# Attention copies per head and ahead of the exponentials, and a shorter routing chain in front of the experts

## The reference, cut to what matters

```python
def attend(q, k, v):
    s = jnp.einsum('bqhgd,bkhd->bhgqk', q, k) * scale
    p = softmax_f32(s).astype(v.dtype)
    return jnp.einsum('bhgqk,bkhd->bqhgd', p, v)
```

```python
p_group = jax.nn.softmax(tf @ w_rg.astype(jnp.float32) + b_rg.astype(jnp.float32), axis=-1)
pg, gsel = lax.top_k(p_group, 1)
...
le_g = jnp.einsum('tge,tg->te', le, jax.nn.one_hot(gsel[:, 0], MOE_GROUPS, dtype=jnp.float32))
pe = jax.nn.softmax(le_g, axis=-1)
pv, pi = lax.top_k(pe, EXPERT_TOPK)
wts = pg * pv / jnp.sum(pv, axis=-1, keepdims=True)
```

## Time and profile before

| | us |
|---|---|
| median of 3 runs | 2212.93 |
| lowest and highest run | 2212.61, 2214.05 |
| the profiled execution | 2210.14 |
| its span, first to last instruction | 2208.2 |
| PE busy in the span | 2006.7 |

### The profile page before, as it was taken

The page is one execution under the profiler, slowest core; times in us unless marked ns, Lnnn a source line. Parts: engine busy times, 40 slices in busy tenths (PEclk is TensorE's granted clock), DMA queues, the critical chain, the costliest instruction groups (busy, mean ns, idle before and its releaser), DMA issues.

```text
span 2208.2 us, 27501 instructions
## 1 busy us (share of the span) xinstructions
PE 2006.7 (91%) x10057; PEld 1407.3 (64%) x10057; DVE 1040.5 (47%) x2098; ACT 559.3 (25%) x1112; POOL 60.0 (3%) x69
## 2 busy tenths in 40 slices
PE   6999898789959999979978989999999878999997
PEld 4888686557736555545445468888544455678886
DVE  3456571356332222243666777777688234423311
ACT  3334300152021111131156033332000224434410
POOL 0000000000001000000000000101000010000000
PEclk8999999899979999989989989999999989999999
DMA  9354472503439999830000512223575011034451
GB/s 384 140 211 196 185 282 86 209 1 119 198 146 368 425 424 422 360 134 0 23 17 6 204 57 85 86 95 128 205 277 199 10 51 48 20 114 152 152 202 45
DMA packets 39463, 357.18 MB, mean 162 GB/s; under 512 B 4295, under 2 KB 9038, under 8 KB 10318
## 3 DMA queue, kind: packets, MB, share of 16 engines
q1 hardware_dynamic: 39374, 355.97, 41.4%
HBM read 354.91 MB, written 1.05 MB: 161 GB/s over the span
## 4 chain that ended last, share of the span: by engine, by line
PE 85%; DVE 4%; ACT 4%; issue 2%; DMA 2%; DVEq 1%; PEld 1%; PEldq 1%; SPq 0%; ACTq 0%
PE bank L641 47%; PE bank L1291 12%; PE bank L1098 6%; PE bank L1084 3%; PE bank L1120 3%; PE bank L744 2%; PE bank L667 2%; PE bank L1263 1%; ACT ring L1398 1%; DMA ring<-in_ada 1%; DVE ring L1894 1%; ACT ring L1407 1%; DVE rstd L1820 1%; ACT hn L1370 1%; PE bank L1186 1%
## 5 line engine op out<-in xcount | busy, mean ns | idle before, releaser
L641 PE MATMUL bank<-hn,ring 128*128 128x256 f32 (+1 forms) x2080 | 524.6, 413 | 13.5 <-ACT hn L1370 9.7
L641 PE MATMUL bank<-arena,ring 128*128 128x256 f32 (+2 forms) x1600 | 471.6, 453 | 25.1 <-issue 13.4
L641 PEld LDWEIGHTS bank<-hn,ring 128*128 128x128 f32 x2080 | 402.3, 194 | 123.9 <-issue 67.7
L641 PEld LDWEIGHTS bank<-arena,ring 128*128 128x128 f32 (+1 forms) x1600 | 301.8, 191 | 191.0 <-issue 154.8
L1291 PE MATMUL bank<-hn,ring 128*128 128x256 f32 x704 | 161.0, 382 | 6.2 <-ACT hn L1370 6.2
L1291 PEld LDWEIGHTS bank<-hn,ring 128*128 128x128 f32 x704 | 134.6, 191 | 25.6 <-issue 7.0
L1800 DVE SCALAR_TENSOR_TENSOR bank<-ring,c_rows 128x1024 f32<-128x1024 f32 x96 | 118.2, 1231 | 34.6 <-DMA ring<-in_ada 29.3
L1291 PE MATMUL bank<-ring 128*128 128x256 f32 x528 | 123.8, 385 | 3.2 <-DVEq L2521 3.2
L1358 ACT ACTIVATE hn<-resid 128x256 f32<-128x256 f32 (+1 forms) x64 | 30.0, 493 | 351.4 <-DVE resid L1879 343.6
L1800 DVE SCALAR_TENSOR_TENSOR ring<-ring,c_rows 128x1024 f32<-128x1024 f32 x96 | 117.2, 1221 | 0.0
L1291 PEld LDWEIGHTS bank<-ring 128*128 128x128 f32 x528 | 101.5, 193 | 18.8 <-issue 3.9
(11 more groups left out here) (381 smaller groups left out, 2156.8 us busy)
## 6 DMA issues: line engine op xcount, KB each, us to landing
ring<-in_ada SPq DMA_DIRECT2D x28, 2048.0 KB, 8.5
ring<-in_up SPq DMA_DIRECT2D x44, 1024.0 KB, 4.9
ring<-in_egu SPq DMA_DIRECT2D x20, 2048.0 KB, 11.1
ring<-in_edn SPq DMA_DIRECT2D x39, 1024.0 KB, 9.7
ring<-in_down SPq DMA_DIRECT2D x16, 1408.0 KB, 9.6
arena<-in_egu SPq DMA_DIRECT2D x10, 2048.0 KB, 11.0
hn<-in_egu SPq DMA_DIRECT2D x9, 2048.0 KB, 10.9
ring<-in_adat SPq DMA_DIRECT2D x8, 2048.0 KB, 12.7
```

What stands on the lines that cost most here:

```text
L641: last = mm(out, lhs(i), rhs(i), start=i == 0, stop=i == k - 1)
```

## The change

In the attention functions ACT copies the transposes of pair p-2 before the exponentials of pair p, and in two instructions, one for each head, each with its own count of `att_PT`; PE waits for each head's bank by itself. In the routing the projection runs with the router weights as stationary operand (8 matmuls of 256 columns, 36 rows out) while the shifted blocks arrive, before the phase ends; DVE copies it out, PE transposes it back in two transposes. DVE picks the experts from the logits themselves, so that no exponential stands ahead of the choice; a running sum over the experts (`fewer`) gives the starts, and one group of three matmuls gives the positions. The weights of the experts, the counts for overfull experts and their tables come behind `pick`. The first expert reads `xs` directly.

```diff
@@ -737,16 +739,16 @@
...
                         pe.wait_ge(s["att_scaled"], done + t + 1)
-                        if t >= 1:
-                            pe.wait_ge(s["att_PT"], done + t)
                         for e in range(2):
+                            if t >= 1:
+                                pe.wait_ge(s["att_PT"], 2 * (done + t) + (e - 1))
                             for x, c in enumerate(pairs[t].tiles):
...
                         g = v // per
-                        pe.wait_ge(s["att_PT"], done + v + 1)
+                        pe.wait_ge(s["att_PT"], 2 * (done + v + 1))
                         if v % per == 0 and g >= 2:
@@ -1035,34 +1037,40 @@
...
-            normed()
+            dot(bank[6][0:NG + NE, 0:T], lambda k: w_route[:, k, :], lambda k: hn_block(k)[:, 0:T], KD).then_inc(s["route_pe"], 1)
...
+            pe.wait_ge(s["route_dve"], 1)
...
-                last = dot(bank[0][:, t * 36:(t + 1) * 36], lambda k: hn[:, k, t * P:(t + 1) * P],
-                           lambda k: w_route[:, k, :], KD)
+                last = tr(bank[0][:, t * 36:(t + 1) * 36], logits[0:NG + NE, t * P:(t + 1) * P], ident[0:NG + NE, 0:NG + NE])
...
-            pe.wait_ge(s["route_dve"], 3)
-            mm(bank[1][:, 0:NE], C("trix"), selm[:, 0, :], start=True, stop=True)
-            mm(bank[1][:, NE:2 * NE], C("trix"), selm[:, 1, :], start=True, stop=False)
-            mm(bank[1][:, NE:2 * NE], ones, selm[:, 0, :], start=False, stop=True)
-            dot(bank[1][0:NE, 2 * NE:2 * NE + 1], lambda t: selm[:, t, :], lambda t: ones[:, 0:1], TT).then_inc(s["route_pe"], 1)
-            pe.wait_ge(s["route_dve"], 4)
-            mm(bank[0][:, 0:NE], cnt[0:NE, 0:1].to_broadcast([NE, P]), C("trix", NE)[:, 0:NE], start=True, stop=True)
-            mm(bank[0][0:NE, NE:NE + 2], C("trix", NE)[:, 0:NE], cnt[0:NE, :], start=True, stop=True).then_inc(s["route_pe"], 1)
-
-            pe.wait_ge(s["moe_G"], 1)
+            pe.wait_ge(s["route_dve"], 2)
+            below = fewer[:, 0:NE]
+            mm(bank[1][:, 0:2 * NE], ones, below.unsqueeze(1).to_broadcast([P, TT, NE]), start=True, stop=False)
+            mm(bank[1][:, 0:2 * NE], C("trix"), selm.rearrange("p t e -> p (t e)"), start=False, stop=False)
+            mm(bank[1][:, NE:2 * NE], ones, selm[:, 0, :], start=False, stop=True).then_inc(s["route_pe"], 1)
+            mm(bank[7][:, 0:NE], ones, below, start=True, stop=True)
+            mm(bank[7][0:NE, NE:NE + 1], below, ones[:, 0:1], start=True, stop=True)
+            mm(bank[7][0:NE, NE + 1:NE + 2], sel_both, ones[:, 0:1], start=True, stop=True).then_inc(s["route_pe"], 1)
+
...
-                dot(bank[2 + k % 4][:, :], lambda t: h_tok[:, t, k * P:(k + 1) * P], lambda t: pick[:, t, :], TT) \
-                    .then_inc(s["moe_X"], 1)
+                for t in range(TT):
+                    if k == 0:
+                        pe.wait_ge(s["moe_G"], t + 1)
+                    last = mm(bank[2 + k % 4][:, :], h_tok[:, t, k * P:(k + 1) * P], pick[:, t, :], start=t == 0, stop=t == TT - 1)
+                last.then_inc(s["moe_X"], 1)
+                if k == 4:
+                    pe.wait_ge(s["route_dve"], 4)
+                    mm(bank[7][0:NE, NE + 2:NE + 3], C("trix", NE)[:, 0:NE], cnt[0:NE, 1:2], start=True, stop=True) \
+                        .then_inc(s["route_pe"], 1)
@@ -1089,13 +1097,14 @@
...
-                    pe.wait_ge(s["moe_xt"], i + 1)
+                    if i >= 1:
+                        pe.wait_ge(s["moe_xt"], i)
...
-                            last = mm(bank[x][64 * q:64 * q + 64, 0:T], x_t[x][:, k, :],
+                            last = mm(bank[x][64 * q:64 * q + 64, 0:T], x_t[x][:, k, :] if i else xs[:, k, 0:CAP],
@@ -1387,6 +1396,14 @@
...
+                    if p >= 2:
+                        t = p - 2
+                        w = pairs[t].branches * pairs[t].w
+                        if t >= 2:
+                            act_e.wait_ge(s["att_O"], done + t - 1)
+                        for e in range(2):
+                            act_e.wait_ge(s["att_T"], 2 * (done + t) + (e + 1))
+                            fn(probs_t[t % 2][:, e, 0:w], banks[:, 4 + e, 0:w], ACT.Copy).then_inc(s["att_PT"], 1)
@@ -1398,13 +1415,6 @@
...
-                    if p >= 2:
-                        t = p - 2
-                        w = pairs[t].branches * pairs[t].w
-                        act_e.wait_ge(s["att_T"], 2 * (done + t + 1))
-                        if t >= 2:
-                            act_e.wait_ge(s["att_O"], done + t - 1)
-                        fn(probs_t[t % 2][:, :, 0:w], banks[:, 4:6, 0:w], ACT.Copy).then_inc(s["att_PT"], 1)
@@ -1572,11 +1582,11 @@
...
-            act_e.wait_ge(s["route_dve"], 1)
-            fn(g4b, g4a, ACT.Exp).then_inc(s["route_act"], 1)
-            act_e.wait_ge(s["route_dve"], 2)
-            fn(e8b, e8a, ACT.Exp).then_inc(s["route_act"], 1)
...
+                if k == 1:
+                    act_e.wait_ge(s["route_dve"], 3)
+                    fn(g4b, g4a, ACT.Exp)
+                    fn(t2d, t2d, ACT.Exp).then_inc(s["route_act"], 1)
@@ -1731,7 +1741,7 @@
...
-            for i in range(ITEMS):
+            for i in range(1, ITEMS):
@@ -2180,6 +2190,10 @@
...
+            V.tensor_copy(logits[0:NG + NE], bank[6][0:NG + NE, 0:T])
+            ve.drain().then_inc(s["route_dve"], 1)
+            V.memset(fewer[:, 0:1], 0.0)
+            ve.wait_ge(s["route_pe"], 2)
@@ -2188,9 +2202,8 @@
...
-                V.tensor_tensor(key, x, b2(top, m), ALU.is_equal)
-                ve.drain()
-                V.tensor_tensor(key, key, rev.unsqueeze(1).to_broadcast([P, 2, m]), ALU.mult)
+                for t in range(2):
+                    V.scalar_tensor_tensor(key[:, t, :], x[:, t, :], top[:, t, :], rev, ALU.is_equal, ALU.mult)
@@ -2202,80 +2215,66 @@
...
+            og = g4c.unsqueeze(3).to_broadcast([P, 2, NG, EPG])
+            V.tensor_tensor(e32, el.rearrange("p t (g e) -> p t g e", g=NG), og, ALU.mult)
+            ve.drain()
+            V.tensor_reduce(e8c, e32.rearrange("p t g e -> p t e g"), AX.X, ALU.add)
+            ve.drain()
+            first_max(e8c, C("rev8"), t2b, e8a, e8d, EPG)
+            V.scalar_tensor_tensor(e8b, e8d, NEG, e8c, ALU.mult, ALU.add)
+            ve.drain()
+            first_max(e8b, C("rev8"), t2c, e8a, e8e, EPG)
+            for dst, src in ((sel_a, e8d), (sel_b, e8e)):
+                V.tensor_tensor(dst.rearrange("p t (g e) -> p t g e", g=NG), og,
+                                src.unsqueeze(2).to_broadcast([P, 2, NG, EPG]), ALU.mult)
+            ve.drain()
+            V.tensor_tensor(selm, sel_a, sel_b, ALU.add)
+            ve.drain()
+            V.tensor_tensor(sel_both, selm[:, 0, :], selm[:, 1, :], ALU.add)
+            ve.drain()
+            V.tensor_tensor_scan(fewer[:, 1:NE + 1], ones[:, 0:NE], sel_both, 0.0, ALU.mult, ALU.add)
+            ve.drain().then_inc(s["route_dve"], 1)
+            ve.wait_ge(s["route_pe"], 3)
+            for chosen, at in ((sel_a, pos_a), (sel_b, pos_b)):
+                for t in range(2):
+                    V.scalar_tensor_tensor(pos[:, t, :], chosen[:, t, :], 1.0, bank[1][:, t * NE:(t + 1) * NE], ALU.mult, ALU.mult,
+                                           accum_out=at[:, t, :])
+                ve.drain()
+            ve.wait_ge(s["moe_iota"], 16)
+            for t in range(2):
+                V.tensor_scalar(pick[:, t, :], iota, pos_a[:, t, :], None, ALU.is_equal)
+                ve.drain()
+                V.scalar_tensor_tensor(pick[:, t, :], iota, pos_b[:, t, :], pick[:, t, :], ALU.is_equal, ALU.add)
+                ve.drain().then_inc(s["moe_G"], 1)
+
             V.tensor_tensor(g4a, gl, b2(t2a, NG), ALU.subtract)
+            V.tensor_tensor(t2d, t2c, t2b, ALU.subtract)
             ve.drain().then_inc(s["route_dve"], 1)
...
+            n_e, over_e = cnt[0:NE, 0:1], cnt[0:NE, 1:2]
+            ve.wait_ge(s["route_pe"], 4)
+            V.tensor_copy(start, bank[7][:, 0:NE])
+            V.tensor_copy(firsts[0:NE, 0:1], bank[7][0:NE, NE:NE + 1])
+            V.tensor_copy(n_e, bank[7][0:NE, NE + 1:NE + 2])
+            ve.drain()
+            V.tensor_copy(offset_i.bitcast(I32), start)
+            V.tensor_scalar(over_e, n_e, float(CAP), None, ALU.is_gt)
+            for most in range(2 * CAP, T, CAP):
+                ve.drain()
+                V.scalar_tensor_tensor(over_e, n_e, float(most), over_e, ALU.is_gt, ALU.add)
             ve.drain().then_inc(s["route_dve"], 1)
             ve.wait_ge(s["route_act"], 1)
             V.tensor_reduce(t2a, g4b, AX.X, ALU.add)
...
-            ve.wait_ge(s["route_act"], 2)
...
-            first_max(e8b, C("rev8"), t2b, e8c, e8d, EPG)
-            V.scalar_tensor_tensor(e8b, e8d, -2.0, e8b, ALU.mult, ALU.add)
-            ve.drain()
-            first_max(e8b, C("rev8"), t2c, e8c, e8e, EPG)
...
-            ve.wait_ge(s["route_pe"], 2)
-            n_e, over_e = cnt[0:NE, 0:1], cnt[0:NE, 1:2]
```

(19 more changed lines are left out.)

48 lines of the change are left out of this document (9 added, 39 removed).

## The result

The changed kernel takes 2175.07 us (median of 2171.53, 2172.11, 2178.03 and 2179.90) beside 2212.77 us of the kernel before: a ratio of 0.9832, with a 95% interval of 0.9807 to 0.9856. It gained 37.7 us where 30 were forecast, and lies just under the range's lower end of 2176. The profiled execution, though, is the slowest of the four, 2179.90 with a span of 2178.0. Against before's profiled 2210.14 it gained 30.2 us, the forecast sum. So the question behind the result is where the other 7.5 us are, and why the runs fall into two groups.

What follows compares the result with a forecast made beforehand. PE bounds the kernel, 85% of the span ending on it. Sparse 7.0, grouped-query 7.4, latent 1.5 and routing 14.1 sum to 30.0 us, taking the median 2212.93 to 2182.9, forecast 2183; range 2176 to 2191.

Steps and rivals of the forecast that it cites:

- Where the waits go, and what is late next: Attention: copies-first ends PE's waits for ACT's copies; DVE's scaling is late next, seven grouped-query waits of 0.6 us, 4.2 staying.
- the ring on ACT: Attention: ACT's exponentials of pair p wait in a loop on pair p-2, 5.5 us over two pairs; 2218 us, chance 0.02.
- Two copies for one, and PE's second wait: Attention: second ACT copy adds 0.2 us, hidden by PE's work; PE's wait between heads costs 0, bound 3 us.
- The clock at the sparse attention's end: Sparse attention's end: with half the idle time gone, full clock stays; transposes give back 0.5 us, values about 0.8.
- The latent attention: Latent attention: 1.5 us gained, from 1.78 at its end and 0.2 beside, less 0.5 for scaling; bounds 0 and 1.78.
- Routing: 14.1 forecast: Norm to first expert: gather starts 12.7 us earlier, less 0.25 for a small matmul, plus 1.7 at the first expert.
- 1.7 us by `xs`: First expert: reading `xs` directly, its matmuls begin at the last copy's end instead of behind GpSimd's gather, 1.7 us gained.
- The first: Rival, routing: PE's closer work keeps full clock in gather (1.7 us) and projection (up to 3.4); 2179.6 us, chance 0.14.
- The second: Rival, attention: DVE's scaling takes ACT's place in more iterations, half of the 15.9 us stays; 2191 us, chance 0.15.
- the third: Rival, experts: the routing gain is given back to the weight streams, DMA being busy there; 2197 us, chance 0.04.
- the fourth: Rival, attention: the slower side, a loop of waits on ACT eating up the routing gain; 2218 us, chance 0.02.
- The rule that was weighed: Routing: the Trainium skill says PE transposes do not count as activity, so the gather begins at half clock; sum stays 30.0.

Runs made afterwards that it cites:

- the split alone: The changed kernel with ACT's copies still per head, but behind the next exponentials as in the kernel before; 2189.37 us, ratio 0.9897.
- the last version: The changed kernel with the scaling's signal given per head and fillers sized a little under PE's idle time at each place; 2158.48 us, ratio 0.9766.

## Why the prediction was right or wrong, point by point

- **Where the waits go, and what is late next: right.** The waits for the copies vanished in all three attentions. The forecast put seven waits of 0.6 us, 4.2 together, in the grouped-query attention; there are seven of at most 0.6, 3.9 together. The stage gained 7.3 to 7.4 us (7.4). That this agrees so well is in part luck: all waits of PE for copies and scaling there fell by 8.2 us, from 12.1 (the 11.6 of the earlier trace rows and 0.5 for the scaling, which the forecast left out). In the sparse attention PE's waits for copies and scaling went from 8.2 us (7.1 of it for the copies of the earlier trace rows) to 2.4, in the latent one from 2.0 to 0.5: 5.8 and 1.5, where the sum had 5.7 and 1.5. The order was the main cause, as the forecast had it; that the split alone takes a quarter of the waits for the copies away was not in it. DVE did not take ACT's place beyond that, and the ring on ACT did not form.
- **Two copies for one, and PE's second wait: right.** The attentions with one copy are 0.5 to 0.8 us longer, not shorter, and no wait between the heads shows.
- **The clock at the sparse attention's end: the step that failed.** The mechanism was right and the size of its term wrong. The forecast said "the clock should stay at full; the transposes give back 0.5 and the values behind them, slowed in the same ratio, about 0.8". That the clock stays was right; the 1.3 us were read from one profile in which it came back soon, and only as far as the end of the attention. In the second profile of before it stayed at half through the first 16 records of the out projection, and both profiles have more half clock in the 90 us behind the attention than the changed kernel. The fillers at that place, which remove the clock loss and leave the wait, gained 6.4 us by the medians. With the 90 us behind it, the stage gained 10.1 us against the first profile and 13.7 against the second. Of these 5.8 are waits and 1.0 is what PE gains beyond them where one goes. So the clock's term was 3.2 to 6.9 us, not 1.3; whether the 1.6 us that lie 60 us behind the wait in the first profile come from it is not shown.
- **The latent attention: the wait right, the clock missed.** The wait gained 1.5 us; the stage gained 3.2 or 4.3, above the upper bound of 1.78. Counted from its first scores it went from 72.5 us to 69.4 or 66.5. The rest is clock, which the sum did not have as a term at all.
- **Routing: 14.1 forecast, 12.5 to 13.2 measured.** Projection 6.41 us (6.9), two transposes, copy and signals 1.0 (1.1), choice from 612.58 to 618.95, 6.4 (5.8), positions 1.5 and 0.8 (1.5 and 0.9), first `pick` 1.5 (1.25): the gather starts 24.84 us behind the sums, before 37.38, so 12.5 (12.7). The gather was 16.84 us long (15.75 + 0.25): 5.0 us of it ran at half clock instead of 3.5. With fillers ahead of it, at full clock, it took 14.85. 1.7 us by `xs`: confirmed to 0.01.
- **The sum against the median.** The stages that the change touches gained more than the 30.0 us of the sum, 33.8 in the first pair of profiles and 37.8 in the second. The others lost 3.5 in the first pair and gained 0.9 in the second, where the sum had 0; in both pairs 1.2 were lost to the wait for DVE in the feed-forward part. Profiled against profiled the sum holds, 30.2 for 30.0, but by luck: before's first profile is at 2210.1, below most of its runs, and the changed kernel's is of the slower group, in which stages that the change does not touch take 7.8 us more than in the quicker one. The forecast knew one execution of each stage and took its clock as a constant of the kernel.
- **The rivals.** The first came true in neither profile of the changed kernel itself, but in part in those of its variants: the projection ran at full clock in one, with the stage 3.7 us shorter where 3.4 were put on it, and for a part of the time in two others. It looked only at the routing. The second, the third and the fourth did not come true; for the third, the experts took 278.68 to 278.69 us in every profile. The rule that was weighed beside it made no difference to the time: between the token transposes and the gather PE idles 4.6 and 1.6 us, and the gather began at half clock in each profile without fillers ahead of it. The reading of the row, that the transposes brought the clock back, is not borne out either. In before's trace the projection ahead of them and they themselves ran at half clock, and the clock rose as they ended; in the kernel with 54 fillers ahead of the out projection the same matmuls and transposes left it at half. From 2.1 us behind them its clock was 0.50, with PE idle:

```profile
646.00:650.00 4.00, 0.00 (x0) 0.00 (x0) 1.68 (x11) 1.69 (x4) 0.00 (x0) 0.50 0.94 399
```

- **Open.** Why DVE's sum comes late in the feed-forward part with the new routing, and why that kernel has more half clock in later stages. Both are reproducible, and a delay of 6 or 12 us does not make them; an earlier start, or another place of the weight transfers, was not tried. Also open is what decides between the two groups: two profiles show where the clock differs, not why.

## What to carry to other kernels

An idle piece of PE can cost its own length and then a stretch at half clock behind it, which here cost more than the wait itself (behind a wait of 2.46 us another 3.2 to 6.9 us, 6.4 by the medians). Put that stretch into the sum as a term with both ends, from more than one profile if there is one, and take the gain of removing such a wait to be the larger for it. Where the wait can't go, idle time filled with unneeded matmuls a little shorter than the gap buys the clock back; fillers longer than the gap give a part or all of it away again (in the routing 2.6 us were gained instead of 5.4, over all the places nothing).

## What the runs showed of the hardware

- The same instructions behind the same idle time (3.46 us) took 6.61, 6.41, 6.41, 6.40, 6.39, 5.03, 4.97 and 3.64 us in the eight profiles with the new routing and no filler ahead of them: the length of the idle time alone does not fix the clock behind it.
- Matmuls of 128 columns whose results nobody reads, in PE's idle time, kept TensorE at full clock behind it; with 38 of them in the routing and 147 elsewhere the mean granted clock was 0.981 in the last version, beside 0.962 and 0.967 in the changed kernel.
- Such a matmul of 128 by 128 in float32 is two instructions in the trace and took 0.23 to 0.27 us at full clock, by the length of the group, while a transpose of the same size is one instruction of 0.12 us (16 in 1.97).
